# A decoder layer on one core: compressed probabilities copied earlier, the second scan a slot later, keys turned once, and another order of the first loads and weight splits

## The chip, the core and the metric

The kernel runs on one core of a Trainium2 chip. The core has a matrix engine (TensorE, "PE" in the profile; its weight loads are "PEld"), a vector engine (VectorE, "DVE"), a scalar engine (ScalarE, "ACT"), a general engine (GpSimd, "POOL") and a queue engine (SyncE, "SP"). The metric is device time in microseconds; the kernel before takes 485.9 us, the median of three runs.

## The reference

One layer of a hybrid decoder on x of 256 rows by 1024 columns, all in float32. An RMS norm, one wide projection, then two token mixers side by side: a gated linear recurrence behind a short convolution, and attention of 16 heads (64 columns each, 4 key groups) with three branches: compressed, selected and window. With 256 rows the selection takes all blocks, so the last two are two plain causal attentions with keys of their own. The mixers are merged by gates, projected, added to x, and a gated feed-forward follows.

```
h = rmsnorm(x, norm1[l]);  z = h @ w_in[l]
xr = causal_conv(z_rx, conv_w, conv_b)
xr = rg_lru(xr, ...)                 # h[t] = a[t] * h[t-1] + u[t], a scan over the rows
y_a = (xr * gelu(z_ry)) @ w_rg_out
k_s, k_w = rmsnorm(z_ks), rmsnorm(z_kw)
p_c = masked_softmax(q @ kc);  o_c = p_c @ vc        # compressed branch, 15 keys
p_s, p_w = the same over 256 keys each
o = g0 * o_c + g1 * (p_s @ v_s) + g2 * (p_w @ v_w)
x = x + (mg0 * y_a + mg1 * (o @ w_nsa_out)) @ w_o
x = x + (silu(h2 @ w_gate) * (h2 @ w_up)) @ w_down,  h2 = rmsnorm(x, norm2)
```

## The kernel before

All weights come as one stream of 73 slots of 128x2048 float32 (1 MB each), in the order of `ORDER`: rx 0 to 3, kk 4 and 5, rg 6 and 7, kc 8, vc 9, qa 10 and 11, qb 12 and 13, vv 14 and 15, ry 16 to 19, then mga, rgo, mgb, nso, wo, gu and dn. SP loads slot i into one of three `raw` buffers. ACT copies it rounded into `w_hi` (L369), DVE puts the remainder raw - w_hi into `w_lo` (L671), and PE makes three products per tile: high by high, high by low, low by high. Each engine's program is one loop over the slots, written out in order; nothing is scheduled by a tool. What the engines tell one another goes by semaphores: `landed`, `hi_ready`, `lo_ready`, `slot_done`, and for the eight PSUM banks `acc_free` (banks 0 to 3, projections) and `misc_free` (banks 4 to 7, transposes and attention).

**The start.** The rows of x come in two tiles of 128: tile 0 from SP's queue, tile 1 from ACT's. ACT squares and sums tile 0 (L375), DVE tile 1 (L679); DVE takes one mean for both (L676), POOL one power (L340), DVE scales both tiles into `xn` (L688). PE turns `xn` with 16 transposes (L1251). Ahead of them it transposes the identity 28 and 6 times (`keep_busy`, L1240), behind them 6 times. ACT writes the high part of the eight turned chunks (L389), DVE the low part (L720). The first slot of weights is loaded and split in two halves (L377 and L379 on ACT, L690 and L729 on DVE). PE's first product `first_x` (L1267 to L1269) takes chunk k as soon as its low part is there.

**The keys.** At slot 7 DVE normalises the keys and writes each 64-column key twice side by side (L892), so that the 16 transposes behind slot 7 (L1511) give keys on partitions 0 to 63 and again on 64 to 127. ACT and DVE then take high and low parts of all 128 partitions (L522, L943) into `k_hh` and `k_ll`. The scores need both copies, since a query holds its high part in the lower and its low part in the upper 64 partitions.

**The heads.** HEAD0 is slot 16; head h is handled at slot 16 + h and after. On PE, slot 16 + h begins with `scores(h)` (L1283). In the middle of its projection stand the transposes of the probabilities of head h - 1 (`turn_a` L1292, `turn_b` L1302); every second slot ends with `values(pair)` (L1319, L1323, L1326). DVE masks the scores and takes their maxima (L808, L811), ACT the exponentials (four, L473), DVE scales them (L844 to L850), and after PE has turned them ACT copies them back (L461, L463). The compressed branch of all heads is done once: scores in `first_y` at slot 16, softmax on DVE and ACT at slot 17, its transposes (L1200, `compressed_transposed`) in the middle of slot 18. ACT copies these into `pcT` (L481), and `values(0)` at the end of slot 18 waits for that copy. In ACT's order the copy stands behind the exponentials of head 2. The recurrence's scans of rows (L1012, four per half) stand on DVE at slot 13 and at slot 17 (`RG_SCAN`), at the end of the slot's work.

Of the kernel before, what the change touches and what calls it, by code (L numbers as in the profile page):

```python
# [59 lines left out]
MISC_ORDER = [("xT", 4), ("ng", 1), ("ngT", 1), ("kT", 4), ("hid", 1), ("kcn", 1), ("qTa", 2), ("vrep", 1), ("qTb", 2), ("att", 4 * HEADS), ("mT", 4), ("hT2", 4)]  # L60
# [12 lines left out]
RG_SCAN = (FIRST["qa"] + 3, FIRST["ry"] + 1)  # L73
# [17 lines left out]
def hybrid_layer(nc, x, stream, small_w, params, out):  # L91
    ctx = ExitStack()
    with ctx:
# [112 lines left out]
        x_in, x1_in, small_in, prm_in, x_again = sem("x_in"), sem("x1_in"), sem("small_in"), sem("prm_in"), sem("x_again")  # L206
# [16 lines left out]
        kn_ready, qn_ready = sem("kn_ready"), sem("qn_ready")  # L223
        sq_summed = sem("sq_summed")
# [11 lines left out]
        merged = sem("merged")  # L236
        x1_ready, silu_ready, a_prod, a_hi_ready, a_lo_ready = sem("x1_ready"), sem("silu_ready"), sem("a_prod"), sem("a_hi_ready"), sem("a_lo_ready")
# [24 lines left out]
        RS_BEFORE = [0, 1, 3, 5, 7, 8]  # L262
# [15 lines left out]
        def _(sp):  # L278
            sp.dma_start(xs[:, 0, :], x[0:P, :]).then_inc(x_in, 16)
# [32 lines left out]
        def _(pool):  # L312
# [45 lines left out]
        def _(sc):  # L358
            sc.dma_start(xs[:, 1, :], x[P:2 * P, :]).then_inc(x1_in, 16)
# [14 lines left out]
            sc.wait_ge(x_in, 16)  # L374
# [18 lines left out]
            chunks_hi(MISC["xT"], 0, G1)  # L393
# [29 lines left out]
            for i in range(NSLOT + 2):  # L423
# [93 lines left out]
                if i == FIRST["kk"] + 4:  # L517
                    for g in range(GROUPS):
                        m = MISC["kT"] + g
                        sc.wait_ge(misc_done, misc_count(m))  # L520
                        for b in range(2):
                            ins = sc.activation(k_hh[:, g, b * S:(b + 1) * S], misc(m)[:, b * S:(b + 1) * S], ACT.Copy,  # L522
                                                scale=prm[:, KN + 1 + b:KN + 2 + b])
                        ins.then_inc(evac_hi, 1)
# [133 lines left out]
        def _(ve):  # L658
# [23 lines left out]
            ve.wait_ge(dve_chain, chain[0])
            ve.wait_ge(squares, 1)
            mean(NORM_X, 1.0 / D)
            ve.wait_ge(rs_ready, rs_count(NORM_X))
            ve.wait_ge(x_in, 16)
# [40 lines left out]
            chunks_lo(MISC["xT"], 0, G1, 0, 4)  # L727
# [38 lines left out]
            for i in range(NSLOT + 2):  # L766
# [120 lines left out]
                if i == FIRST["kk"] + 3:  # L887
                    for t in range(T2):
# [49 lines left out]
                if i == FIRST["kk"] + 4:  # L938
                    for g in range(GROUPS):
                        m = MISC["kT"] + g  # L940
                        ve.wait_ge(evac_hi, g + 1)
                        for b in range(2):
                            ins = ve.scalar_tensor_tensor(out=k_ll[:, g, b * S:(b + 1) * S], in0=misc(m)[:, b * S:(b + 1) * S],  # L943
                                                          scalar=prm[:, KN + 1 + b:KN + 2 + b],
                                                          in1=f(k_hh[:, g, b * S:(b + 1) * S]), op0=ALU.mult, op1=ALU.subtract)
                        ins.then_inc(misc_free[m % 4], 1)
# [60 lines left out]
                for v in range(2):  # L1007
                    if i == RG_SCAN[v]:
# [4 lines left out]
                        link(ins)  # L1013
# [92 lines left out]
        def _(pe):  # L1106
# [531 lines left out]
```

## Time and profile before

| | us |
|---|---|
| median of 3 runs (485.82 to 485.99) | 485.9 |
| the profiled execution's own time | 487.44 |
| its span | 485.7 |
| PE busy in the span | 478.0 (98%) |
| DVE busy | 355.0 (73%) |
| ACT busy | 279.8 (58%) |
| POOL busy | 15.1 (3%) |

The profile is of one execution. Busy times are counted from the records, and PE's matmuls overlap one another, so that a busy PE does not say that nothing could be taken away. The granted clock of TensorE (PEclk) is given as a share of full speed.

### The profile page before, as it was taken

What the parts mean: (1) busy time and instruction counts of PE and PEld (TensorE: products, weight loads), DVE (VectorE), ACT (ScalarE), POOL (GpSimd) and SP (SyncE); (2) the same over time, 40 slices, a digit from 0 to 9 for tenths busy, and PEclk for the clock granted to TensorE, in tenths of its full rate; (3) what the DMA queues carried; (4) which work ended last, traced back from release to release, by engine and by line L of the source; (5) the groups of instructions that cost most, each with busy time, mean ns of one, the idle gap of its engine ahead of it and who ended that gap; (6) DMA issues with size and microseconds to landing.
All of it is one profiled execution on the core that took longest, in us unless ns stands there. A gap on an engine that the chain in (4) does not pass through costs nothing.

```text
span 485.7 us, 7347 instructions
## 1 busy us (share of the span) xinstructions
PE 478.0 (98%) x2803; PEld 412.7 (85%) x2803; DVE 355.0 (73%) x630; ACT 279.8 (58%) x451; POOL 15.1 (3%) x25
## 2 busy tenths in 40 slices
PE   7999999999989999999999999999999999999997
PEld 7998998788979778877787888888888888888886
DVE  3999899789895887757763767787777777754332
ACT  4755986675765896566763335755555445453320
POOL 2000200220000000000000000000000000000000
PEclk9999999999998999999999999999999999999999
DMA  8745966424224245333344362564555445554402
GB/s 311 272 162 208 373 271 255 174 88 173 88 97 164 88 173 194 152 128 135 106 154 165 104 251 88 188 246 177 187 206 209 175 173 181 200 224 175 173 1 86
DMA packets 12833, 84.73 MB, mean 174 GB/s; under 512 B 1536, under 2 KB 1792, under 8 KB 3072
## 3 DMA queue, kind: packets, MB, share of 16 engines
q1 hardware_dynamic: 12096, 82.32, 46.8%
q0 software_dynamic: 272, 1.05, 0.6%
q10 hardware_dynamic: 432, 0.91, 0.5%
q8 instruction: 22, 0.36, 0.3%
q14 instruction: 11, 0.09, 0.1%
HBM read 83.22 MB, written 1.05 MB: 173 GB/s over the span
## 4 chain that ended last, share of the span: by engine, by line
PE 93%; DVE 4%; ACT 2%; issue 0%; POOL 0%; POOLq 0%; DVEq 0%
PE bank L1109 18%; PE bank L1111 18%; PE bank L1110 18%; PE bank L1147 16%; PE bank L1150 8%; PE bank L1283 2%; PE bank L1319 2%; PE bank L1240 2%; PE bank L1521 1%; PE bank L1292 1%; DVE w_lo L671 1%; PE bank L1326 1%; PE bank L1323 1%; PE bank L1367 1%; ACT pbuf L473 1%; PE bank L1302 1%
## 5 line engine op out<-in xcount | busy, mean ns | idle before, releaser
L671 DVE TENSOR_TENSOR w_lo<-raw,w_hi 128x2048 fp32r<-128x2048 f32 x71 | 162.5, 2289 | 49.8 <-ACT w_hi L369 49.4
L369 ACT ACTIVATE w_hi<-raw 128x2048 fp32r<-128x2048 f32 x72 | 138.0, 1917 | 48.7 <-PE bank L1111 46.2
L1147 PE MATMUL bank<-h_hl,w_hi 128*128 128x512 f32 x336 | 80.3, 391 | 0.0
L1147 PEld LDWEIGHTS bank<-h_hl,w_hi 128*128 128x128 f32 x336 | 61.7, 188 | 11.9
L1109 PE MATMUL bank<-w_hi,h_hl 128*128 128x512 f32 x160 | 63.6, 398 | 0.0
L1111 PE MATMUL bank<-w_hi,h_hl 128*128 128x512 f32 x160 | 62.5, 390 | 0.0
L1110 PE MATMUL bank<-w_lo,h_hl 128*128 128x512 f32 x160 | 62.4, 390 | 0.0
L1109 PE MATMUL bank<-w_hi,act 128*128 128x512 f32 x150 | 59.1, 394 | 0.0
L1111 PE MATMUL bank<-w_hi,act 128*128 128x512 f32 x150 | 58.5, 390 | 0.0
L1110 PE MATMUL bank<-w_lo,act 128*128 128x512 f32 x150 | 58.4, 390 | 0.0
L1150 PEld LDWEIGHTS bank<-h_hl,w_lo 128*128 128x128 f32 x336 | 43.1, 191 | 1.6
L1150 PE MATMUL bank<-h_hl,w_lo 128*128 128x256 f32 x336 | 43.6, 283 | 0.0
L497 ACT ACTIVATE scr<-bank 128x512 f32<-128x512 f32 x22 | 13.1, 598 | 49.9 <-PE bank L1147 49.9
L1109 PE MATMUL bank<-h_hl,w_hi 128*128 128x256 f32 x128 | 36.6, 286 | 0.0
L1111 PE MATMUL bank<-h_hl,w_lo 128*128 128x256 f32 x128 | 36.2, 283 | 0.0
L1110 PE MATMUL bank<-h_hl,w_hi 128*128 128x256 f32 x128 | 36.2, 283 | 0.0
L1111 PEld LDWEIGHTS bank<-w_hi,h_hl 128*128 128x128 f32 x160 | 30.0, 188 | 6.5
L1109 PEld LDWEIGHTS bank<-w_hi,h_hl 128*128 128x128 f32 x160 | 30.1, 188 | 6.2 <-issue 0.4
L1110 PEld LDWEIGHTS bank<-w_lo,h_hl 128*128 128x128 f32 x160 | 30.1, 188 | 5.8
L1109 PEld LDWEIGHTS bank<-w_hi,act 128*128 128x128 f32 x150 | 28.2, 188 | 6.1 <-issue 0.4
L1111 PEld LDWEIGHTS bank<-w_hi,act 128*128 128x128 f32 x150 | 28.1, 188 | 6.0
L1110 PEld LDWEIGHTS bank<-w_lo,act 128*128 128x128 f32 x150 | 28.2, 188 | 5.6
(244 smaller groups left out, 744.6 us busy)
## 6 DMA issues: line engine op xcount, KB each, us to landing
raw<-stream_dram SPq DMA_DIRECT2D x72, 1024.0 KB, 4.8
w<-stream_dram SPq DMA_DIRECT2D x4, 1024.0 KB, 8.6
raw<-stream_dram SPq DMA_DIRECT2D x2, 512.0 KB, 7.3
xs<-x_dram POOLq DMA_DIRECT2D x1, 1024.0 KB, 5.4
out_dram<-xs SPq DMA_DIRECT2D x3, 256.0 KB, 2.0
xs<-x_dram ACTq DMA_DIRECT2D x1, 512.0 KB, 5.1
xs<-x_dram SPq DMA_DIRECT2D x1, 512.0 KB, 4.8
scr<-small_dram ACTq DMA_DIRECT2D x1, 320.0 KB, 8.8
```

The lines of the kernel that those rows point to most:

```text
L369: sc.activation(w_hi[:, i % HL, :], raw[:, i % RAW, :], ACT.Copy).then_inc(hi_ready, 1)
L473: ins = sc.activation(prob[:, a:b], bank[:, off:off + b - a], ACT.Exp, bias=ast[:, 1, j:j + 1], scale=SCALE, accum_out=ast[:, 2, j:j + 1])
L497: sc.activation(gus[:, j % 2, :, :], gate_up(j)[:, :, S:2 * S], ACT.Copy).then_inc(gu_low, 1)
L671: ve.tensor_tensor(w_lo[:, i % HL, :], raw[:, i % RAW, :], f(w_hi[:, i % HL, :]), ALU.subtract).then_inc(lo_ready, 1)
L1109: pe.matmul(out_, l_hi, r_hi, start=start, stop=False)
L1110: pe.matmul(out_, l_hi, r_lo, start=False, stop=False)
L1111: return pe.matmul(out_, l_lo, r_hi, start=False, stop=stop)
L1147: ins = pe.matmul(acc(u + mt)[:, :], w_hi[:, s, c:c + P], a_hl[:, k, :, :].rearrange("p x s -> p (x s)"), start=n == 0, stop=n == 2 * KC - ...
L1150: ins = pe.matmul(acc(u + mt)[:, 0:S], w_lo[:, s, c:c + P], a_hl[:, k, 0, :], start=n == 0, stop=n == 2 * KC - 1, skip_group_check=True)
L1240: pe.transpose(psum[3][:, 0:P], ident[:, :], ident[:, :])
L1283: ins = pe.matmul(o3, q, kt[:, g, :].rearrange("p (b c) -> p b c", b=2)[:, :, 0:w], start=n == 0, stop=n == 1)
L1319: pe.matmul(o[e], v_sb[:, 0, b * S + g * DH:b * S + (g + 1) * DH], pTa[e][:, b * S:(b + 1) * S], start=b == 0, stop=False)
```

## The change

Five things change. In ACT's order at slot 18 the copy into `pcT` moves ahead of the copies of the turned probabilities and of the exponentials. The second half of the scans moves from slot 17 to slot 18, with a semaphore `scanned` for which ACT's first copy of attention output waits (it writes over what the scan reads). The keys are no longer written twice: 8 transposes in place of 16, high and low parts on 64 partitions, and two transfers from POOL's queue that copy partitions 0 to 63 of `k_hh` and `k_ll` to 64 to 127; `scores(0)` waits for both. Each tile of x is loaded in two halves of 64 partitions, one from each queue, tile 0 first, and has a mean and a power of its own; tile 1's squares are summed half on DVE and half on ACT. The first half of the first weights is split in two quarters, the second half is copied by ACT between chunks 3 and 4 of the turned x, and only 2 identity transposes stand behind the transposes of x.

```
-MISC_ORDER = [("xT", 4), ("ng", 1), ("ngT", 1), ("kT", 4), ...
+MISC_ORDER = [("xT", 4), ("ng", 1), ("ngT", 1), ("kT", 2), ...
-RG_SCAN = (FIRST["qa"] + 3, FIRST["ry"] + 1)
+RG_SCAN = (FIRST["qa"] + 3, FIRST["ry"] + 2)
 # SP
-            sp.dma_start(xs[:, 0, :], x[0:P, :]).then_inc(x_in, 16)
+            for t in range(T2):
+                sp.dma_start(xs[0:64, t, :], x[t * P:t * P + 64, :]).then_inc(x_in[t], 16)
 # POOL
-            rsqrt(NORM_X)
+            for t in range(T2):
+                rsqrt(NORM_X, t, 1)
             for t in range(T2):
                 rsqrt(NORM_K, t, 8)
+            for g in range(2):
+                wait_misc_read(pool, MISC["kT"] + g)
+            for n, kt in enumerate((k_hh, k_ll)):
+                pool.dma_start(kt[64:128, :, :], kt[0:64, :, :]).then_inc(k_doubled[n], 16)
 # ACT
-            sc.dma_start(xs[:, 1, :], x[P:2 * P, :]).then_inc(x1_in, 16)
+            for t in range(T2):
+                sc.dma_start(xs[64:128, t, :], x[t * P + 64:(t + 1) * P, :]).then_inc(x_in[t], 16)
...
+            sc.wait_ge(x_in[1], 32)
+            sc.activation(scr[:, 3584:4096], xs[:, 1, 512:1024], ACT.Square, accum_out=ss[:, NORM_X, 2:3]).then_inc(x1_square, 1)
             sc.wait_ge(first_half, 16)
-            sc.activation(w_hi[:, 0, 0:1024], raw[:, 0, 0:1024], ACT.Copy).then_inc(hi_half, 1)
-            sc.wait_ge(landed[0], 16)
-            sc.activation(w_hi[:, 0, 1024:2048], raw[:, 0, 1024:2048], ACT.Copy).then_inc(hi_ready, 1)
+            for e in range(2):
+                sc.activation(w_hi[:, 0, e * 512:(e + 1) * 512], raw[:, 0, e * 512:(e + 1) * 512], ACT.Copy).then_inc(hi_half, 1)
...
-            chunks_hi(MISC["xT"], 0, G1)
+            chunks_hi(MISC["xT"], 0, G1, 0, 4)
+            sc.wait_ge(landed[0], 16)
+            sc.activation(w_hi[:, 0, 1024:2048], raw[:, 0, 1024:2048], ACT.Copy).then_inc(hi_ready, 1)
+            chunks_hi(MISC["xT"], 0, G1, 4, KC)
...
+                if i == HEAD0 + 2:
+                    u = USE["pcT"]
+                    sc.wait_ge(pcT_done, 1)
+                    sc.activation(pcT[:, :, :].rearrange("p a s -> p (a s)"), acc(u)[:, :], ACT.Copy).then_inc(acc_free[u % 4], 1)
                 if h >= 3 and h % 2 == 1 and h <= HEADS + 1:
                     pair = (h - 3) // 2
+                    if pair == 0:
+                        sc.wait_ge(scanned, 2)
 # DVE
-            ve.wait_ge(x1_in, 16)
-            ve.scalar_tensor_tensor(out=scr[:, 3072:4096], in0=xs[:, 1, :], ...
+            ve.wait_ge(squares, 1)
+            ve.tensor_scalar(ms[:, NORM_X, 0:1], ss[:, NORM_X, 0:1], 1.0 / D, EPS, ALU.mult, ALU.add).then_inc(ms_ready, 1)
+            ve.wait_ge(x_in[1], 32)
+            ve.scalar_tensor_tensor(out=scr[:, 3072:3584], in0=xs[:, 1, 0:512], ...
+            ve.wait_ge(x1_square, 1)
...
-            chunks_lo(MISC["xT"], 0, G1, 0, 4)
+            chunks_lo(MISC["xT"], 0, G1, 0, 2)
+            first_quarter(1)
+            chunks_lo(MISC["xT"], 0, G1, 2, 4)
...
-                        ve.tensor_tensor(kn[:, t, :].rearrange("p (c e d) -> p c e d", c=8, e=2),
-                                         kz[:, t, :].rearrange("p (c d) -> p c d", c=8).unsqueeze(2).broadcast_to([P, 8, 2, DH]),
+                        ve.tensor_tensor(kn[:, t, 0:512].rearrange("p (c d) -> p c d", c=8),
+                                         kz[:, t, :].rearrange("p (c d) -> p c d", c=8),
...
-                        link(ins)
+                        ins.then_inc(scanned, 1)
+                        ve.wait_ge(scanned, v + 1)
 # PE
-            keep_busy(6)
+            keep_busy(2)
...
                 for k in range(KC):
+                    if k == KC // 4:
+                        pe.wait_ge(lo_half, 2)
...
                 if h == 0:
                     wait_misc_read(pe, MISC["qTa"] + 1)
+                    for x in range(2):
+                        pe.wait_ge(k_doubled[x], 16)
```

The rows below are the engines' instructions in program order: the line, the operation, the tile written and the tiles read. ACT around the copy into `pcT` (slots 17 to 19), before; L434 and L448 belong to other work of these slots, L461 and L463 copy turned probabilities, L473 are exponentials, L369 is a weight copy:

```order
L369 ACTIVATE w_hi<-raw 128x2048
L434 ACTIVATE scr<-bank 128x512
L461 ACTIVATE pbuf<-bank 128x512
L463 ACTIVATE pbuf<-bank 128x256
L473 ACTIVATE pbuf,ast<-bank,ast 128x128 x2
L473 ACTIVATE pbuf,ast<-bank,ast 128x256 x2
L481 ACTIVATE pcT<-bank 128x512
L369 ACTIVATE w_hi<-raw 128x2048
```

The same place on ACT after the change (L379 is now the weight copy, L467 the copy into `pcT`, L493 the exponentials):

```order
L379 ACTIVATE w_hi<-raw 128x2048
L448 ACTIVATE scr<-bank 128x512
L467 ACTIVATE pcT<-bank 128x512
L481 ACTIVATE pbuf<-bank 128x512
L483 ACTIVATE pbuf<-bank 128x256
L493 ACTIVATE pbuf,ast<-bank,ast 128x128 x2
L493 ACTIVATE pbuf,ast<-bank,ast 128x256 x2
L379 ACTIVATE w_hi<-raw 128x2048
```

The copy into `pcT` moved up past four exponentials and two copies. DVE at slots 17 and 18 before: the weights' low part (L671), the scans (L1012), then the maxima of head 2 (L808, one instruction and one reading of its result per tile) and the rest of that slot:

```order
L671 TENSOR_TENSOR w_lo<-raw,w_hi 128x2048
L1012 SCALAR_TENSOR_TENSOR xs<-scr 128x256 x4
L808 ISA bank,ast<-bank,maskf 128x128
...
L811 TENSOR_SCALAR ast<-ast 128x4
L671 TENSOR_TENSOR w_lo<-raw,w_hi 128x2048
L844 RECIPROCAL ast<-ast 128x4
L845 TENSOR_TENSOR ast<-ast,gates 128x4
L850 TENSOR_SCALAR pbuf<-pbuf,ast 128x128 x2
L850 TENSOR_SCALAR pbuf<-pbuf,ast 128x256 x2
L808 ISA bank,ast<-bank,maskf 128x128
```

DVE at the same place after (L688 is the low part, L1042 the scans, L836 and L839 the maxima, L872 to L878 the scaling of the probabilities):

```order
L688 TENSOR_TENSOR w_lo<-raw,w_hi 128x2048
L836 ISA bank,ast<-bank,maskf 128x128
...
L839 TENSOR_SCALAR ast<-ast 128x4
L688 TENSOR_TENSOR w_lo<-raw,w_hi 128x2048
L872 RECIPROCAL ast<-ast 128x4
L873 TENSOR_TENSOR ast<-ast,gates 128x4
L878 TENSOR_SCALAR pbuf<-pbuf,ast 128x128 x2
L878 TENSOR_SCALAR pbuf<-pbuf,ast 128x256 x2
L1042 SCALAR_TENSOR_TENSOR xs<-scr 128x256 x4
L836 ISA bank,ast<-bank,maskf 128x128
```

The four scans moved from ahead of the maxima of head 2 to ahead of those of head 3. DVE at the start of the program before (L688 scales x, L690 and L729 are the low halves of the first weights, L720 the low parts of the turned chunks):

```order
L688 TENSOR_SCALAR scr<-xs,rs 128x1024 x2
L690 TENSOR_TENSOR w_lo<-raw,w_hi 128x1024
L720 SCALAR_TENSOR_TENSOR h_hl<-bank,prm,h_hl 128x256 x4
L729 TENSOR_TENSOR w_lo<-raw,w_hi 128x1024
L720 SCALAR_TENSOR_TENSOR h_hl<-bank,prm,h_hl 128x256 x4
```

DVE at the start after (L708 scales x, L713 are the quarters, L757 the second half, L746 the chunks):

```order
L708 TENSOR_SCALAR scr<-xs,rs 128x1024 x2
L713 TENSOR_TENSOR w_lo<-raw,w_hi 128x512
L746 SCALAR_TENSOR_TENSOR h_hl<-bank,prm,h_hl 128x256 x2
L713 TENSOR_TENSOR w_lo<-raw,w_hi 128x512
L746 SCALAR_TENSOR_TENSOR h_hl<-bank,prm,h_hl 128x256 x2
L757 TENSOR_TENSOR w_lo<-raw,w_hi 128x1024
L746 SCALAR_TENSOR_TENSOR h_hl<-bank,prm,h_hl 128x256 x4
```

The second quarter now stands between chunks 1 and 2. On ACT, in the same way, the copy of the second half of the first weights, which stood ahead of the eight chunks, now stands between chunk 3 and chunk 4.

## Rows read from the trace of the kernel before

**Rows 1.** The page's chain that ended last, shares of the span by engine.

```profile
PE 93%; DVE 4%; ACT 2%; issue 0%; POOL 0%; POOLq 0%; DVEq 0%
```

**Rows 2.** Waits of PE, 0 to 160 us: who waits for whom, total us, times, longest.

```profile
PE bank L1319 <- ACT pcT L481: 2.1, 1, 2.1
```

**Rows 3.** Timeline of PE, 130 to 160 us: start, us, engine, line, operation.

```profile
138.17 0.60 PE L1200 MATMUL bank<-ident,scr 128*128 128x128 f32 x4
...
142.02 0.28 PE L1111 MATMUL bank<-h_hl,w_lo 128*128 128x256 f32 x1
144.36 1.18 PE L1319 MATMUL bank<-pbuf,v_sb 128*64 128x256 f32 x8 [2.07 <-ACT pcT L481]
...
155.03 0.87 PE L1283 MATMUL bank<-act 128*128 128x256 f32 x4
```

**Rows 4.** Timeline of ACT, 130 to 160 us.

```profile
139.74 0.38 ACT L463 ACTIVATE pbuf<-bank 128x256 f32<-128x256 f32 x1
142.01 0.37 ACT L473 ACTIVATE pbuf<-bank,ast 128x128 f32<-128x128 f32 x1 [1.90 <-DVE ast L811]
...
143.61 0.61 ACT L481 ACTIVATE pcT<-bank 128x512 f32<-128x512 f32 x1
...
154.04 0.50 ACT L473 ACTIVATE pbuf<-bank,ast 128x256 f32<-128x256 f32 x1
```

**Rows 5.** Timeline of DVE, 130 to 160 us.

```profile
137.94 2.43 DVE L1012 TENSOR_TENSOR_SCAN xs<-scr 128x256 f32<-128x256 f32 x4
...
141.89 2.28 DVE L671 TENSOR_TENSOR w_lo<-raw,w_hi 128x2048 fp32r<-128x2048 f32 x1
...
144.49 1.01 DVE L850 TENSOR_SCALAR pbuf<-pbuf,ast 128x128 f32<-128x128 f32 x4
```

**Rows 6.** Stretches: length; busy of PE, PEld, DVE, ACT, POOL; PEclk; DMA.

```profile
144.36:148.80 4.44, 4.44 (x26) 3.47 (x27) 1.72 (x9) 2.53 (x3) 0.00 (x0) 0.62 0.59 240
162.04:164.84 2.80, 2.80 (x26) 2.10 (x26) 1.89 (x8) 2.80 (x10) 0.00 (x0) 1.00 0.78 260
```

**Rows 7.** Timeline of PE, 60 to 63 us.

```profile
60.24 1.91 PE L1511 MATMUL bank<-ident,scr 128*128 128x128 f32 x16
61.91 0.36 PE L1109 MATMUL bank<-h_hl,w_hi 128*128 128x256 f32 x1
```

**Rows 8.** The page's DMA issues: KB each, us from issue to landing.

```profile
w<-stream_dram SPq DMA_DIRECT2D x4, 1024.0 KB, 8.6
...
xs<-x_dram POOLq DMA_DIRECT2D x1, 1024.0 KB, 5.4
```

**Rows 9.** Timeline of SP, whole span, and of PE, 84 to 85 us.

```profile
66.12 0.91 SPq L296 DMA_DIRECT2D w<-stream_dram  x2
...
84.50 0.43 PE L1521 MATMUL bank<-w,pbuf 128*64 128x256 f32 x1
```

**Rows 10.** Timeline of PE, 2 to 18 us.

```profile
2.80 6.78 PE L1240 MATMUL bank<-ident 128*128 128x128 f32 x34 [2.80 <-POOL bd L331]
9.42 1.91 PE L1251 MATMUL bank<-ident,scr 128*128 128x128 f32 x16
...
12.00 0.36 PE L1267 MATMUL bank<-h_hl,w_hi 128*128 128x256 f32 x1
...
17.82 0.28 PE L1109 MATMUL bank<-h_hl,w_hi 128*128 128x256 f32 x1
```

**Rows 11.** Timelines of ACT and then of DVE, 0 to 130 us.

```profile
9.75 1.06 ACT L379 ACTIVATE w_hi<-raw 128x1024 fp32r<-128x1024 f32 x1 [0.84 <-DMA raw<-stream_dram]
10.78 3.03 ACT L389 ACTIVATE h_hl<-bank,prm 128x256 fp32r<-128x256 f32 x8
...
8.15 1.42 DVE L688 TENSOR_SCALAR scr<-xs,rs 128x1024 f32<-128x1024 f32 x2 [0.83 <-POOL rs L340]
...
11.37 1.66 DVE L720 SCALAR_TENSOR_TENSOR h_hl<-bank,prm,h_hl 128x256 fp32r<-128x256 f32 x4 [0.67 <-ACT h_hl L389]
12.95 1.21 DVE L729 TENSOR_TENSOR w_lo<-raw,w_hi 128x1024 fp32r<-128x1024 f32 x1
```

More of the change, by code:

```diff
@@ L205, in hybrid_layer @@
         landed = [sem(f"landed{i}") for i in range(RAW)]
-        x_in, x1_in, small_in, prm_in, x_again = sem("x_in"), sem("x1_in"), sem("small_in"), sem("prm_in"), sem("x_again")
+        x_in = [sem(f"x_in{t}") for t in range(T2)]
+        small_in, prm_in, x_again, x1_square = sem("small_in"), sem("prm_in"), sem("x_again"), sem("x1_square")
         hi_ready, lo_ready = sem("hi_ready"), sem("lo_ready")
@@ L236, in hybrid_layer @@
         merged = sem("merged")
+        scanned = sem("scanned")
         x1_ready, silu_ready, a_prod, a_hi_ready, a_lo_ready = sem("x1_ready"), sem("silu_ready"), sem("a_prod"), sem("a_hi_ready"), sem("a_lo_ready")
@@ L518, in _ @@
                     for g in range(GROUPS):
-                        m = MISC["kT"] + g
+                        m = MISC["kT"] + g // 2
+                        src = slice(64 * (g % 2), 64 * (g % 2) + 64)
                         sc.wait_ge(misc_done, misc_count(m))
                         for b in range(2):
-                            ins = sc.activation(k_hh[:, g, b * S:(b + 1) * S], misc(m)[:, b * S:(b + 1) * S], ACT.Copy,
-                                                scale=prm[:, KN + 1 + b:KN + 2 + b])
+                            ins = sc.activation(k_hh[0:64, g, b * S:(b + 1) * S], misc(m)[src, b * S:(b + 1) * S], ACT.Copy,
+                                                scale=prm[src, KN + 1 + b:KN + 2 + b])
                         ins.then_inc(evac_hi, 1)
@@ L676, in mean, with first_quarter @@
                 ve.tensor_scalar(ms[0:p, n, 0:w], ss[0:p, n, 0:w], scale, EPS, ALU.mult, ALU.add).then_inc(ms_ready, 1)
-            ve.wait_ge(x1_in, 16)
-            ve.scalar_tensor_tensor(out=scr[:, 3072:4096], in0=xs[:, 1, :], scalar=1.0, in1=xs[:, 1, :], op0=ALU.mult,
+            ve.wait_ge(squares, 1)
+            ve.tensor_scalar(ms[:, NORM_X, 0:1], ss[:, NORM_X, 0:1], 1.0 / D, EPS, ALU.mult, ALU.add).then_inc(ms_ready, 1)
+            ve.wait_ge(x_in[1], 32)
+            ve.scalar_tensor_tensor(out=scr[:, 3072:3584], in0=xs[:, 1, 0:512], scalar=1.0, in1=xs[:, 1, 0:512], op0=ALU.mult,
                                     op1=ALU.mult, accum_out=ss[:, NORM_X, 1:2]).then_inc(dve_chain, 1)
             chain[0] += 1
[L682 to L686, printed above, removed]
+            ve.wait_ge(x1_square, 1)
+            link(ve.tensor_scalar(ss[:, NORM_X, 3:4], ss[:, NORM_X, 2:3], 1.0 / D, EPS, ALU.mult, ALU.add))
+            ve.scalar_tensor_tensor(out=ms[:, NORM_X, 1:2], in0=ss[:, NORM_X, 1:2], scalar=1.0 / D, in1=ss[:, NORM_X, 3:4],
+                                    op0=ALU.mult, op1=ALU.add).then_inc(ms_ready, 1)
             for t in range(T2):
+                ve.wait_ge(rs_ready, rs_count(NORM_X, t))
+                ve.wait_ge(x_in[t], 32)
                 ve.tensor_scalar(xn[:, t, :], xs[:, t, :], rs[:, NORM_X, t:t + 1], None, ALU.mult).then_inc(xn_ready, 1)
-            ve.wait_ge(hi_half, 1)
-            ve.tensor_tensor(w_lo[:, 0, 0:1024], raw[:, 0, 0:1024], f(w_hi[:, 0, 0:1024]), ALU.subtract).then_inc(lo_half, 1)
+            def first_quarter(e):
+                ve.wait_ge(hi_half, e + 1)
+                ve.tensor_tensor(w_lo[:, 0, e * 512:(e + 1) * 512], raw[:, 0, e * 512:(e + 1) * 512],
+                                 f(w_hi[:, 0, e * 512:(e + 1) * 512]), ALU.subtract).then_inc(lo_half, 1)
+            first_quarter(0)
             ve.wait_ge(prm_in, 16)
@@ L939, in _ @@
                     for g in range(GROUPS):
-                        m = MISC["kT"] + g
+                        m = MISC["kT"] + g // 2
+                        src = slice(64 * (g % 2), 64 * (g % 2) + 64)
                         ve.wait_ge(evac_hi, g + 1)
                         for b in range(2):
[L943 to L946, printed above, removed]
+                            ins = ve.scalar_tensor_tensor(out=k_ll[0:64, g, b * S:(b + 1) * S], in0=misc(m)[src, b * S:(b + 1) * S],
+                                                          scalar=prm[src, KN + 1 + b:KN + 2 + b],
+                                                          in1=f(k_hh[0:64, g, b * S:(b + 1) * S]), op0=ALU.mult, op1=ALU.subtract)
+                        if g % 2 == 1:
+                            ins.then_inc(misc_free[m % 4], 1)
                 if i == FIRST["qa"] + 2:
@@ L1504, in _ @@
                     pe.wait_ge(kn_ready, 2)
-                    for g in range(GROUPS):
-                        m = MISC["kT"] + g
+                    for v in range(2):
+                        m = MISC["kT"] + v
                         wait_misc_free(pe, m)
```

19 lines of the change are left out of this document (8 added, 11 removed).

## The prediction

> **What bounds the kernel now.** First the page: the chain that ended last is PE for 93% of the span [rows 1], so only what shortens PE's own work or a wait of PE counts. Then PE's waits up to 160 us: beside the one at the very start a single one stands there, 2.1 us of L1319 for ACT's copy into `pcT` [rows 2]. Then the timelines around it. PE's last product of slot 18 starts at 142.02, the next instruction, `values(0)`, at 144.36 [rows 3]. ACT had finished the copies of turned probabilities at 140.12, waited 1.90 us for DVE's maxima of head 2, made four exponentials and only then copied `pcT` at 143.61 [rows 4]. DVE was late with the maxima because the four scans (2.43 us) stood ahead of them [rows 5]. Last the stretches: behind the wait the granted clock was 0.62 on the mean over 4.44 us, that is, part of it at 1.2 GHz in place of 2.4, and the values and scores took 4.44 us; the same group 18 us later took 2.80 us at clock 1.00 [rows 6].
>
> **The copy into pcT, and the scans.** The compressed transposes start at 138.17 and take 0.60 [rows 3], so `pcT` can be copied at 138.8. The copy takes 0.5 to the next start (143.61 to about 144.1, duration 0.61 [rows 4]) and ends before 139.4; the two copies behind it, which ended at 140.12, are put off by at most 0.1. PE then has all that `values(0)` needs at 140.2, and starts it right behind slot 18, at 142.02 + 0.12 = 142.14 (the first slot's 48 such matmuls take 17.82 - 12.00 = 5.82, 0.12 each [rows 10]). Gain: 144.36 - 142.14 = 2.2 us.
>
> Who is late next? `scores(3)` follows the values at 142.14 + 1.9 = 144.0 and needs the banks that the exponentials of head 2 read. Without the scans ahead of them the maxima end where the scans did, at 137.94 + (141.89 - 140.37) = 139.5; the exponentials start behind the copies at 140.2 and take 143.61 - 142.01 = 1.6 [rows 4, 5]: done at 141.8, 2.2 us early. Even at their old time of 143.6 they would be in time. So the first edit alone takes the wait away; the scans' move only makes it safe.
>
> What the move queues: DVE works on the next low part (2.2, from 139.5 to 141.7), scales the probabilities (1.01 [rows 5] and two small steps, 1.4 together by my estimate), done at 143.2, and scans until 145.6. Behind the scans stand the maxima of head 3, until 147.1. The exponentials of head 3 come only after PE has turned head 2 and ACT has copied it, at about 149.0, so 1.9 us are left. ACT's new wait for `scanned` holds its copy of attention output until 145.6 and ends it at 146.0; behind it are the copies of the turned probabilities at 148.2, and on PE `turn_b(2)` at about 148.0, which needs that copy. Both have 2 us. The tightest place is the usual one, the last exponential against `scores(4)`: in the old trace 154.54 against 155.03 [rows 3, 4]. Both shift together. Cost: nothing.
>
> **The clock.** With no gap at 142 there is nothing like what went before the drop. The stretch shrinks from 4.44 to 2.80 [rows 6]: gain 1.6 us. Bounds: 0 if the clock fell for another reason, 1.6 if it stays up. I take 1.6, as this is the only stretch with a low clock and it stands right behind the only gap.
>
> **Keys.** Of the 16 transposes behind slot 7, 1.67 us from start to next start [rows 7], 8 go: gain 0.83 us on PE, where nothing hides them. DVE writes half as much ahead of it, which costs nothing. The high and low parts keep their counts and row lengths; 64 partitions in place of 128 take as long or less. POOL waits for them and starts two transfers of 512 KB; behind it in its queue there are only the powers for q, two slots on. The parts are 16 operations of 0.4 at most behind transposes that end at 61, with other work between them, so I put the transfers at 70. They take 5.4 us by the one POOL transfer of the same total size [rows 8], and `scores(0)` wants them at slot 16, far behind the 84.50 of rows 9. They meet the stream there: two 1 MB loads issued at 66.12, first used at 84.50 [rows 9]. With the 8.6 us of such a load [rows 8] the second (issued at 67.0) lands at 76; if the doubled keys take all 5.4 us from it, at 81, and PE comes at 84.0. Cost: nothing, up to a delay of 8 us.
>
> Here the Trainium skill speaks against the change (SBUF — State Buffer, Door 1: The DMA port swizzle): the memory's DMA ports are divided by partition, and 64 partitions reach only half of them. An estimate by its figure of 436 GB/s for all is 218 GB/s, 4.8 us for the two. No run here shows such a transfer; it is within the 5.4 us taken above, and the sum is the same by either.
>
> **The start.** Tile 0 of x arrives earlier, and its scaled rows too, but does PE wait for them? It runs 34 identity transposes from 2.80 without a gap until the transposes of x at 9.42 [rows 10], while DVE began to scale at 8.15 and had tile 0 at about 8.9 [rows 11]. So PE's own 34 hold the place, they are all kept, and the earlier x is worth nothing. Behind the 16 transposes 4 of 6 go (0.44), which is no gain either, since PE then waits for the first low part. That comes from ACT's chunk 0 (10.78) over DVE (11.37) to PE (12.00), 1.22 us [rows 10, 11]. Chunk 0 waited for the second-half copy, to 10.81 [rows 11], and for the tenth of the 16 transposes (9.42 to 11.33), which ends near 10.7. So it starts at 10.71: 0.07 earlier.
>
> Then the chunks. ACT's go at 0.38 apart (3.03 for eight), DVE's at 0.41 (1.66 for four) [rows 11]. ACT: chunks 0 to 3 until 12.2, second half (1.0) until 13.2, chunk 4 at 13.2. DVE: chunks 0 and 1 from 11.30, second quarter from 12.1 (half of 1.21, so 0.6), chunks 2 and 3 from 12.7, second half 13.5 to 14.7, chunk 4 at 14.7 where before it came behind L729, at 14.1 [rows 11]. PE takes 0.73 per chunk (six matmuls): from 11.93 it comes to chunk 4 at 14.85, but that is ready only at 14.7 + 0.6 (12.00 - 11.37) = 15.3. It ends the slot at 18.2 in place of 17.8. Cost: 0.35 us, taken between the ends below as each step of it has a row. Slot 1 needs its first low half; ACT's copy (1.9) ends at 16.6 and DVE's half at 17.8, in time. ACT and DVE are about 0.9 later for the next slots too; what hides this is that PE waited for no low part anywhere before 142 [rows 2]. Bounds: -1.0 (the whole second-half copy, 1.06, off the way to the first product) to +1.06 (put wholly into it).
>
> **Sum.** -2.2 - 1.6 - 0.83 + 0.35 = -4.3 us. The profiled execution took 487.44 with a span of 485.7, so it should be 483.1 with a span of 481.4. The median of the runs is 1.5 below that execution: 485.9 - 4.3 = 481.6.
>
> **Rivals.**
> (a) The forecast, 481.6; its own range is 480.9 to 482.5. Chance 0.69.
> (b) The start gains in place of losing: ACT's idle time ahead of 9.75 was the real limit, the first product comes 0.8 earlier and the stall at chunk 4 is covered. For it: ACT did wait for a load there (0.84 us) [rows 11]. Against: PE's 34 transposes. -4.65 - 0.8 gives 480.4. Chance 0.11.
> (c) The clock falls somewhere else. The start now has two gaps of PE, 0.5 us ahead of the first product and 0.4 at chunk 4. If they bring one stretch at 1.2 GHz like the one at 144, +1.6: 483.2. Against: the old gap was 2.07 us. Chance 0.11.
> (d) Slower. The doubling of the keys crowds the loads of rows 9: if it delays them by more than 8 us, PE waits at 84 for each us more, and with a wait like the old one the clock drops too (1.6). It decides over the sign when PE waits 4.3 - 1.6 = 2.7 us, with the loads 10.7 us late; a doubling three times as slow as the POOL transfer (16 us) makes it 8 us of waiting: 8 + 1.6 - 4.3 = +5.3, so 491.2. Against: the 1 MB transfers of rows 8 took 5.4 and 8.6 us beside the stream. Chance 0.04.
> (e) The change doesn't do what it says: `values(0)` waits as long as before for something that I take as long done, the rest holds: -0.83 + 0.35 = -0.5, 485.4. The trace shows ACT's `pcT` as the last to come but not how close the second is. Chance 0.05.
>
> **How the numbers follow.** About 0.2% (1 us) is what a measurement of this kernel tells from no change. Faster by more: (a), (b) and (c), 0.91. Within: (e), 0.05. Slower: (d), 0.04. The range 480.2 to 483.8 holds (a), (b) and (c) with their bounds and leaves out (d), (e) and the outer ends of the start, under 0.2 together.
>
> **What would show it.** In the profile after: no wait of PE ahead of L1319 at slot 18, `pcT` copied at about 139 and ahead of the exponentials; PEclk 1.00 around 142 to 148; 8 key transposes in about 0.84 us; the transposes of x still at 9.42 and the first product near 11.9; a gap of 0.4 us in the first slot at chunk 4, and slot 1 starting 0.2 to 0.5 later than at 17.82. I am wrong if the transposes of x start well before 9.4, if a low clock stands anywhere, if PE waits at slot 19 or 20 for DVE's maxima, or if PE waits for `w1` near 84.

## The result and the profile after

The changed kernel takes 484.4 us (483.42 to 485.17, 12 executions). One more execution of it took 602.27 us at a mean granted clock of 0.755 and is left out as slow. Beside it the kernel before took 485.82 to 487.6 over 13 executions. The ratio is 0.9949, 95% interval 0.9937 to 0.9961: faster, by 1.9 to 3.1 us. The forecast was 481.6 with a range of 480.2 to 483.8, so the time lies outside it, 2.8 us above.

The first thing that the runs show is in the kernel before. Its times are not one group. Of its 57 executions beside the experiments below, 29 took 485.85 to 486.31 with a mean granted clock of 1.00, and 28 took 487.46 to 488.06 with 0.996; none lies between. The medians of the two kinds are 486.1 and 487.6. By their times, the three runs given at the outset were all of the first kind (median 485.9), and the profiled execution (487.44) was of the second. The interval above takes both kinds together; against the first kind alone the change gains 1.6 us.

| us | before | after |
|---|---|---|
| profiled execution, own time | 487.44 | 484.29 |
| its span | 485.7 | 482.5 |
| slot 1 begins | 17.82 | 19.08 |
| `values(0)` begins | 144.36 | 142.73 |
| stretch of values and scores ends | 148.80 | 145.58 |

Profile against profile the span is 3.2 us shorter, where 4.3 was forecast. The page's chain after, to be read beside [rows 1]:

```profile
PE 96%; DVE 1%; DMA 1%; ACT 0%; POOL 0%; issue 0%; ACTq 0%; DVEq 0%
```

All waits of PE in the changed kernel, over the whole span. The one of [rows 2] is gone; in its place are three short ones at the start, behind the 2.8 us that both kernels have:

```profile
PE bank L1271 <- POOL bd L335: 2.8, 1, 2.8
PE bank L1300 <- DVE h_hl L746: 0.7, 2, 0.5
PE bank L1282 <- DVE scr L708: 0.4, 1, 0.4
```

Timelines of the changed kernel around slot 18, of ACT, then DVE, then PE, each in a fence of its own; they answer to [rows 3 to 5]. `pcT` is L467, the exponentials L493, the maxima end with L839, `values(0)` is L1352 to L1359, the scores L1316:

```profile
139.31 0.60 ACT L467 ACTIVATE pcT<-bank 128x512 f32<-128x512 f32 x1 [1.54 <-PE bank L1231]
...
140.55 0.38 ACT L493 ACTIVATE pbuf<-bank,ast 128x128 f32<-128x128 f32 x1
...
146.19 0.38 ACT L475 ACTIVATE scr<-bank 128x256 f32<-128x256 f32 x1 [0.89 <-DVE xs L1042]
```

```profile
139.85 0.17 DVE L839 TENSOR_SCALAR ast<-ast 128x4 f32<-128x4 f32 x1
```

```profile
142.53 0.28 PE L1142 MATMUL bank<-h_hl,w_lo 128*128 128x256 f32 x1
142.73 1.08 PE L1352 MATMUL bank<-pbuf,v_sb 128*64 128x256 f32 x8
...
144.62 0.96 PE L1316 MATMUL bank<-act 128*128 128x256 f32 x4
145.42 0.28 PE L1140 MATMUL bank<-h_hl,w_hi 128*128 128x256 f32 x1
```

The values follow slot 18 directly, and ACT's new wait for the scans (0.89 us) holds nothing of PE. The stretch of values and scores took 4.44 us at clock 0.62 [rows 6] and takes 2.85 at 1.00 (columns as in [rows 6]):

```profile
142.73:145.58 2.85, 2.85 (x27) 2.16 (x27) 2.81 (x9) 2.40 (x2) 0.00 (x0) 1.00 0.75 253
```

The start is where the trace departs from the forecast. ACT, then DVE, of the changed kernel (L385 and L387 square tiles 0 and 1, L698 is DVE's half of tile 1, L708 scales):

```profile
5.25 1.06 ACT L385 ACTIVATE scr<-xs 128x1024 f32<-128x1024 f32 x1 [0.52 <-DMA xs<-x_dram]
8.02 0.64 ACT L387 ACTIVATE scr<-xs 128x512 f32<-128x512 f32 x1 [1.62 <-DMA xs<-x_dram]
```

```profile
8.02 0.69 DVE L698 SCALAR_TENSOR_TENSOR scr<-xs 128x512 f32<-128x512 f32 x1 [1.44 <-DMA xs<-x_dram]
9.06 0.75 DVE L708 TENSOR_SCALAR scr<-xs,rs 128x1024 f32<-128x1024 f32 x1
10.25 0.75 DVE L708 TENSOR_SCALAR scr<-xs,rs 128x1024 f32<-128x1024 f32 x1 [0.45 <-POOL rs L344]
```

And PE (L1271 identity, L1282 transposes of x, L1300 first product, L1140 slot 1):

```profile
2.80 6.66 PE L1271 MATMUL bank<-ident 128*128 128x128 f32 x34 [2.80 <-POOL bd L335]
9.87 2.29 PE L1282 MATMUL bank<-ident,scr 128*128 128x128 f32 x16 [0.40 <-DVE scr L708]
...
12.82 0.36 PE L1300 MATMUL bank<-h_hl,w_hi 128*128 128x256 f32 x1 [0.45 <-DVE h_hl L746]
...
16.13 0.36 PE L1300 MATMUL bank<-h_hl,w_hi 128*128 128x256 f32 x1 [0.20 <-DVE h_hl L746]
...
19.08 0.28 PE L1140 MATMUL bank<-h_hl,w_hi 128*128 128x256 f32 x1
```

The kernel before, where ACT had to do with tile 0 and DVE with tile 1, and POOL's first power of the changed kernel:

```profile
5.68 1.06 ACT L375 ACTIVATE scr<-xs 128x1024 f32<-128x1024 f32 x1 [2.17 <-DMA xs<-x_dram]
```

```profile
5.89 1.22 DVE L679 SCALAR_TENSOR_TENSOR scr<-xs 128x1024 f32<-128x1024 f32 x1 [5.89 <-DMA xs<-x_dram]
```

```profile
6.67 0.55 POOL L344 TENSOR_TENSOR rs<-ms,half 128x1 f32<-128x1 f32 x1 [3.92 <-DVE ms L696]
```

Tile 0 is usable at 5.25, a little before the old 5.7, but tile 1 only at 8.02, where before it was at 5.9. Tile 0's power is there at 7.2, yet DVE scales the tile only at 9.06, because tile 1's sum stands ahead of it in DVE's order and waits for tile 1. So the early tile 0 brings nothing. DVE has scaled tile 0 at 9.8 and tile 1 at 11.0, and PE is made to wait. Slot 1 starts 1.26 us later than in [rows 10], not 0.35.

### The profile page after: what moved, and what is told of

Read it like the earlier page. It is cut to its first block, busy times and chain, and to the rows that moved or that the text cites. A ratio compares the mean times of both kernels' runs of the same rounds, so it can differ in the third digit from the quotient of the medians.

```text
span 482.5 us, 7338 instructions
## 1 busy us (share of the span) xinstructions
PE 475.7 (99%) x2791; PEld 410.9 (85%) x2791; DVE 354.5 (73%) x633; ACT 280.7 (58%) x454; POOL 17.1 (4%) x28
## 4 chain that ended last, share of the span: by engine, by line
PE 96%; DVE 1%; DMA 1%; ACT 0%; POOL 0%; issue 0%; ACTq 0%; DVEq 0%
PE bank L1140 19%; PE bank L1141 19%; PE bank L1142 19%; PE bank L1178 16%; PE bank L1181 8%; PE bank L1316 3%; PE bank L1261 2%; PE bank L1352 2%; PE bank L1556 1%; PE bank L1325 1%; DMA xs<-x_dram 1%; PE bank L1400 1%; PE bank L1359 1%; PE bank L1335 1%; PE bank L1356 1%; DVE h_hl L746 0%
## 5 line engine op out<-in xcount | busy, mean ns | idle before, releaser
L688 DVE TENSOR_TENSOR w_lo<-raw,w_hi 128x2048 fp32r<-128x2048 f32 x71 | 162.5, 2290 | 49.5 <-ACT w_hi L379 49.1
L379 ACT ACTIVATE w_hi<-raw 128x2048 fp32r<-128x2048 f32 x72 | 138.0, 1917 | 47.9 <-PE bank L1142 41.5
L1140 PE MATMUL bank<-w_hi,h_hl 128*128 128x512 f32 x160 | 63.6, 398 | 0.0
L1140 PE MATMUL bank<-w_hi,act 128*128 128x512 f32 x150 | 59.1, 394 | 0.0
L513 ACT ACTIVATE scr<-bank 128x512 f32<-128x512 f32 x22 | 13.2, 598 | 49.9 <-PE bank L1178 49.9
L1140 PE MATMUL bank<-h_hl,w_hi 128*128 128x256 f32 x128 | 36.6, 286 | 0.0
L1140 PEld LDWEIGHTS bank<-w_hi,h_hl 128*128 128x128 f32 x160 | 30.1, 188 | 6.2 <-issue 0.4
L1140 PEld LDWEIGHTS bank<-w_hi,act 128*128 128x128 f32 x150 | 28.2, 188 | 6.1 <-issue 0.4
## 6 DMA issues: line engine op xcount, KB each, us to landing
act<-act POOLq DMA_DIRECT2D x2, 512.0 KB, 13.1
```

What stands on the lines that cost most here:

```text
L379: sc.activation(w_hi[:, i % HL, :], raw[:, i % RAW, :], ACT.Copy).then_inc(hi_ready, 1)
L513: sc.activation(gus[:, j % 2, :, :], gate_up(j)[:, :, S:2 * S], ACT.Copy).then_inc(gu_low, 1)
L688: ve.tensor_tensor(w_lo[:, i % HL, :], raw[:, i % RAW, :], f(w_hi[:, i % HL, :]), ALU.subtract).then_inc(lo_ready, 1)
L1140: pe.matmul(out_, l_hi, r_hi, start=start, stop=False)
```

## The experiments

The theory after the result: (1) two kinds of execution of the kernel before, with and without a fall of the clock behind the wait at 142; (2) the start costs 1.3 us, because a tile of x now comes in two pieces of 64 partitions. The rival to (1) is a gain that was smaller than forecast at slot 18, the rival to (2) is the new order of quarters and chunks. Each time is a median. The kernel before ran beside them in three sets, whose first kind has the medians 485.99, 486.07 and 486.07; sets of different kernels are compared on that ground. In the expectations, e1 is the copy alone, e4 all but the start, e6 the changed kernel with whole tiles of x, and e7 the same with halves by column.

**The copy into pcT alone.**

```
+                if i == HEAD0 + 2:        # now ahead of the exponentials
+                    u = USE["pcT"] ...    # the block that stood behind them
```

> The kernel before with one edit: the copy into pcT stands ahead of the exponentials on ACT in slot 18. The scans stay at the end of slot 17, keys and start are as before. Theory T (two modes): the kernel before is at 485.9 in executions whose clock stays up behind the wait at 142, and at 487.5 in those where it drops; this edit takes the 2.2 us wait and with it the drop. Both modes then come to one: 485.9 - 2.2 = 483.7 and 487.5 - 3.8 = 483.7, spread under 0.6. Rival U (the scans' move is needed too): DVE's maxima of head 2 still end at 141.9, the exponentials at 143.6, and scores(3) or a later head waits for them about 1 us: 484.7, with two modes left.

Measured: 483.92 (483.76 to 483.95), one group. Timeline of DVE, ACT and PE in this kernel, in three fences (L811 ends the maxima, L477 begins the exponentials, L1319 is `values(0)`, L1283 the scores):

```profile
141.82 0.17 DVE L811 TENSOR_SCALAR ast<-ast 128x4 f32<-128x4 f32 x1
```

```profile
138.82 0.60 ACT L453 ACTIVATE pcT<-bank 128x512 f32<-128x512 f32 x1 [1.54 <-PE bank L1200]
...
142.03 0.37 ACT L477 ACTIVATE pbuf<-bank,ast 128x128 f32<-128x128 f32 x1 [1.85 <-DVE ast L811]
```

```profile
142.24 1.08 PE L1319 MATMUL bank<-pbuf,v_sb 128*64 128x256 f32 x8
...
144.12 0.97 PE L1283 MATMUL bank<-act 128*128 128x256 f32 x4
```

The scans still stand ahead of the maxima and the exponentials are as late as before, yet nothing on PE waits for them: theory T, not U.

**The second scan alone.**

```
-RG_SCAN = (FIRST["qa"] + 3, FIRST["ry"] + 1)
+RG_SCAN = (FIRST["qa"] + 3, FIRST["ry"] + 2)
```

> The kernel before with the second scan alone a slot later (and ACT's wait for it); the copy into pcT stays behind the exponentials of head 2. Theory T (the copy's place is the cause, but the scans set when the exponentials end): the maxima of head 2 end at 139.6, the exponentials at 141.9, the copy into pcT at 142.5: PE waits about 0.4 us in place of 2.1 and the clock never drops: 484.3, one mode. Rival (the scans' move does nothing by itself, since ACT's exponentials wait for something else): 2.1 us of wait and both modes stay, 485.9 and 487.6.

Measured: 483.94 (483.94 to 484.1), one group, as good as the copy alone. Its rows of ACT and of PE (L484 is the copy, L1323 `values(0)`):

```profile
140.06 0.37 ACT L476 ACTIVATE pbuf<-bank,ast 128x128 f32<-128x128 f32 x1
...
141.64 0.63 ACT L484 ACTIVATE pcT<-bank 128x512 f32<-128x512 f32 x1
```

```profile
142.07 0.28 PE L1115 MATMUL bank<-h_hl,w_lo 128*128 128x256 f32 x1
142.41 1.08 PE L1323 MATMUL bank<-pbuf,v_sb 128*64 128x256 f32 x8
```

I had the copy 0.2 us too late; it ends at 142.27 and PE loses about 0.2. So each of the two edits by itself removes the wait, the scans' move all but these 0.2 us. No kernel with both and nothing else was run; what the scans' move adds to the copy can be bounded by the runs below at under 0.1 us.

**The wait filled.**

```
                 if pair == 0:
+                    for _ in range(18):
+                        pe.transpose(o_bank[:, 0:P], ident[:, :], ident[:, :])
```

> The kernel before with 18 transposes of the identity on PE where it waits for pcT in slot 18; their output is overwritten by the values behind them and changes nothing. They take about 18 x 0.11 = 2.0 us. Theory G (the idle stretch of PE is what precedes the drop of the clock, the late values by themselves are not): the 2.1 us stay lost, but the granted clock is 1.00 in each execution: 485.9 to 486.2, one mode. Rival (the drop comes with what runs at 144, or by chance): two modes, 486.0 and 487.6, about half of the executions each.

Measured: 486.09 (485.86 to 486.19), 12 executions, all at clock 1.00 (0.999 once). The kernel before fell to 0.996 in 9 of 17 beside it. PE, then the stretch of values and scores:

```profile
142.30 2.13 PE L1315 MATMUL bank<-ident 128*128 128x128 f32 x18
144.54 1.08 PE L1321 MATMUL bank<-pbuf,v_sb 128*64 128x256 f32 x8
```

```profile
144.30:148.80 4.50, 4.38 (x40) 3.77 (x39) 3.11 (x17) 2.66 (x4) 0.00 (x0) 1.00 0.71 233
```

The values are as late as before, but PE did not idle and the clock stays at 2.4 GHz. Without the idle stretch the fall does not come; theory G.

**The start alone, the keys alone, and all but the start.** The first two are the kernel before with one group of edits; the third has the copy, the scans and the keys, with the old start.

> The kernel before with the edits of the start alone (x tile by tile in halves of 64 partitions, the quarters, the second-half copy behind chunk 3, two rsqrts, keep_busy 2). Theory S (the start costs what the trace after shows): slot 1 starts at 19.1 in place of 17.82, +1.25 us: 487.1 where the clock stays up at 144 and 488.7 where it drops. Rival S0 (the start costs the 0.35 forecast, and the late slot 1 of the trace after is peculiar to that execution or caught up later): 486.2 and 487.8.

> The kernel before with the edits of the keys alone (8 transposes in place of 16, doubled by two transfers of POOL). Theory K (the doubling slows other loads, but PE hardly waits): 8 transposes save 0.88 us, behind them 0.4 us is lost until w1 at 84.5: -0.45 net, 485.4 or, with the drop at 144, 487.0. Rival K0: the full 0.88 stays, 485.0 or 486.6. Rival K1 (the doubling costs PE a wait at w1): slower than before by 0.5 or more.

> The changed kernel with the start of the kernel before (x in two whole tiles, two halves of the first weights, one rsqrt): pcT, scans and keys changed. Theory S: 484.44 - 1.25 = 483.2, slot 1 at 17.82, no wait of PE and clock 1.00 at 142 to 149. Rival S0: the start costs 0.35 and this gives 484.1. If terms add, it is also e1 plus the keys alone: 483.7 - 0.45 = 483.2.

Measured, start alone: 487.01; nine executions at 486.69 to 487.77 with clock 1.00, three at 488.42 to 488.48 with 0.996. Within the first kind it is 0.9 us slower than before (486.88 against 485.99), and its slot 1 starts at 19.07. Keys alone: 485.33; eight at 485.07 to 485.37, four at 486.79 to 487.01. Its profile (485.07) is of the first kind and shows the wait without the fall: PE, then the stretch of values and scores, which took 4.44 us at clock 0.62 in [rows 6]:

```profile
143.57 1.08 PE L1327 MATMUL bank<-pbuf,v_sb 128*64 128x256 f32 x8 [2.09 <-ACT pcT L486]
```

```profile
143.57:146.43 2.86, 2.86 (x26) 2.34 (x27) 1.53 (x8) 2.42 (x3) 0.00 (x0) 1.00 0.66 203
```

All but the start: 483.02 (482.87 to 483.52). Against the copy alone that is -0.90 for the keys and the scans' move together, and the keys alone give -0.83 (485.16 against 485.99, first kind). So the keys keep nearly all of the 8 transposes' 0.88, theory K0, and the scans' move adds under 0.1. The 0.4 us that I believed lost behind the transposes is not there. In the kernel without the new start PE comes to `w1` at

```profile
83.63 0.43 PE L1535 MATMUL bank<-w,pbuf 128*64 128x256 f32 x1
```

which is 0.87 ahead of [rows 9]. Beside the other edits the start costs 484.4 - 483.0 = 1.4 us, alone 0.9. The profiles of the changed kernel and of all but the start are 1.25 us apart at slot 1 (19.08 against 17.83) and 1.4 at `w1` (85.03 against 83.63). The profile of the start alone is 1.24 behind [rows 9] at `w1` (85.74) as well, but its execution is only 1.1 slower than the median of the first kind, and the median of its nine only 0.9. Where that difference comes from stays open. Theory S holds, S0 falls.

**Only the halves of x.** The kernel before, each tile of x in two transfers:

```
-            sp.dma_start(xs[:, 0, :], x[0:P, :])
+            for t in range(T2):
+                sp.dma_start(xs[0:64, t, :], x[t * P:t * P + 64, :])
                                               # and rows 64 to 127 on ACT's queue
```

> The kernel before with one edit: each tile of x comes in two halves of 64 partitions, one from SP's queue and one from ACT's; all else as before. Theory H (the half-tile transfers are what costs at the start): tile 1 is there at about 8.0 in place of 5.9, and the one rsqrt needs both tiles, so the scaled rows come 2.1 us later; 0.5 of that is covered by PE's identity transposes: slot 1 at about 19.4, +1.6 us, 487.6 where the clock stays up at 144. Rival O (the order of the chunks and quarters costs, not the transfers): 486.0.

Measured: 488.31, from 486.98 to 492.35; six at clock 1.00 have 486.98 to 487.85. PE in the profiled execution (490.73), and its stretches:

```profile
10.38 0.91 PE L1242 MATMUL bank<-ident 128*128 128x128 f32 x6 [1.95 <-POOL rs L341]
11.17 3.57 PE L1253 MATMUL bank<-ident,scr 128*128 128x128 f32 x16
```

```profile
10.30:14.60 4.30, 4.22 (x23) 4.07 (x24) 2.89 (x4) 1.99 (x4) 0.03 (x1) 0.60 1.02 423
```

The other six have 488.78 to 492.35 with clock 0.990 to 0.997. The transfers by themselves do the harm: +1.3 us where the clock stays up (the median of the six at 1.00 is 487.35). Behind the idle 1.95 us there is a second place where it can fall: here the 16 transposes took 3.57 us in place of 1.91 [rows 10]. Theory H, and a cost beyond it.

**Whole tiles, and halves by column.** The changed kernel; first with `xs[:, t, :]` in one transfer per queue, then with

```
-                sp.dma_start(xs[0:64, t, :], x[t * P:t * P + 64, :])
+                sp.dma_start(xs[:, t, 0:512], x[t * P:(t + 1) * P, 0:512])
                                               # and columns 512 to 1023 on ACT's queue
```

> The changed kernel with each tile of x in one transfer of 128 partitions (tile 0 on SP's queue, tile 1 on ACT's); quarters, order of chunks and two rsqrts as in the changed kernel. Theory H: tile 1 is there at 5.9 again, the transposes of x start at 9.4, slot 1 at 18.2: 483.4, with the small scatter of e4. Rival O: the late tile was covered and the order of chunks costs: slot 1 at 19 still, 484.3.

> The changed kernel with each tile of x in two transfers of 128 partitions by 512 columns in place of 64 partitions by 1024: the same two transfers of 256 KB on each of the same two queues. Theory H1 (the 64 partitions cost): as e6, tile 1 at about 6, 483.4. Rival H2 (the number of transfers ahead of the first weights, or both tiles standing in both queues, costs): tile 1 at about 8 as in the changed kernel, 484.4.

Measured: 483.05 (482.79 to 483.36) and 483.17 (482.68 to 483.46). The same stretch, 3 to 7 us, of before, the changed kernel, whole tiles, and column halves, one fence each; the last two columns are DMA share and GB/s:

```profile
3.00:7.00 4.00, 4.00 (x20) 4.00 (x20) 1.11 (x1) 1.67 (x3) 0.00 (x0) 1.00 0.96 350
```

```profile
3.00:7.00 4.00, 4.00 (x20) 4.00 (x20) 0.15 (x1) 2.43 (x3) 0.33 (x1) 1.00 1.02 231
```

```profile
3.00:7.00 4.00, 4.00 (x20) 4.00 (x20) 0.12 (x2) 1.82 (x4) 0.00 (x0) 1.00 0.97 353
```

```profile
3.00:7.00 4.00, 4.00 (x20) 4.00 (x20) 1.15 (x6) 2.88 (x5) 0.55 (x1) 1.00 0.98 316
```

In all four the DMA engines are busy throughout, but in the second they move a third less, in the fourth a tenth less. Two transfers of 256 KB on each queue are in both the second and the fourth; only the shape differs, so it is the 64 partitions (H1), not the number of transfers (H2) nor the order of the chunks (O). Nor is it the length of a row, which is 4 KB in the whole tiles too. A small part comes ahead of the transfer: to issue one took 0.56 to 0.85 us with 64 partitions and 0.40 to 0.47 with 128. By columns DVE has tile 1 as early as before:

```profile
5.92 0.69 DVE L698 SCALAR_TENSOR_TENSOR scr<-xs 128x512 f32<-128x512 f32 x1 [0.17 <-DMA xs<-x_dram]
```

With whole tiles the new start is worth nothing: 483.05 against 483.02 with the old one.

**Fewer identity transposes.** Column halves, and in front of x:

```
-            keep_busy(28)    # and 6 behind the first rsqrt
+            keep_busy(22)    # and 2
```

> The changed kernel with x in column halves (as e7) and 24 of PE's identity transposes ahead of x in place of 34. In e7 tile 0 of x is scaled by 7.7 and tile 1 by 8.9, but PE is at its identity transposes until 9.23. Theory I (PE's own transposes hold the start once x lands early): the 16 transposes of x end at 9.9 in place of 11.0, the first product comes at 10.8, slot 1 at 17.1 to 17.5, as the first weights' second half allows: 482.4 to 482.7. Rival J (the first weights' copies hold it): slot 1 stays at 18.0, 483.1. Rival C (the gap ahead of x drops the clock at the start in some executions): two modes, 482.6 and 484.0 or more.

Measured: 482.09, five executions: 481.82, 482.03, 482.09, 482.8 and 483.97. The profile is of the slowest. There PE turned x from 7.98, but then waited, because ACT had no weights:

```profile
11.85 0.36 PE L1300 MATMUL bank<-h_hl,w_hi 128*128 128x256 f32 x1 [1.60 <-DVE h_hl L746]
```

```profile
9.59 1.15 ACT L390 ACTIVATE w_hi<-raw 128x512 fp32r<-128x512 f32 x2 [3.17 <-DMA raw<-stream_dram]
```

Slot 1 began at 18.10 there, no earlier than with column halves alone (18.06), and a further wait of 0.64 us stands near 103, for DVE's `cmpr`. So J holds in that execution. Theory I fits the median, but of an execution as fast no trace was taken, so that its place is not shown. No clock below 0.999 was seen; the profiled execution kept 1.00 behind its 1.60 us of idle PE. It is the fastest version measured, 0.9901 of before (0.9883 to 0.9919), though its executions spread by 2 us.

## Why the prediction was wrong

Two steps failed. Together they are 1.6 + (1.4 - 0.35) = 2.65 of the 2.8 us.

**"The median of the runs is 1.5 below that execution: 485.9 - 4.3."** The sum was made against a profiled execution of 487.44 and carried over to a median of another kind. The clock term (1.6) was real, and its size was right: the medians of the two kinds differ by 487.6 - 486.1 = 1.5, and the stretch by 4.44 - 2.86 = 1.6. But it can be gained only from executions that lose it, and the three with median 485.9 had not. The 1.5 us between them and the profile was the term itself, in plain sight. Against 486 the copy saves 2.1 (483.92), against 487.6 it saves 3.7; both kinds end at 483.9.

**"... the earlier x is worth nothing ... Cost: 0.35 us."** The start was taken as a question of order, with x in its halves arriving no later than the whole tiles. The working never priced the four transfers, although it had a rule for them in hand. What the runs showed is 231 GB/s in place of 350, tile 1 at 8.02 in place of 5.9, and 1.4 us lost. The part that was worked out is about right: with x in column halves the first product comes at 11.81 and slot 1 at 18.06 (forecast 11.93 and 18.2), with the waits of 0.46 and 0.20 us at chunks 0 and 4. The bounds, up to +1.06, were drawn from ACT's copies and so missed the cause. The Trainium skill has it (SBUF — State Buffer, "Can I just issue two DMAs to hit both halves?"): a transfer to partitions from 0 and one to partitions from 64 issued together gain almost nothing over one, only a single transfer over all 128 reaches every port. By that page's 218 GB/s for 64 partitions (Door 1) the 1 MB of x is an estimated 4.8 us of transfer. The trace agrees: over 3 to 7 us, 231 GB/s in the changed kernel and 230 in the one with only the halves. I had weighed that section for the keys, where there was room, and not for x, where there was none.

The other steps:

- The wait: right. Gone, with the copy done early; the first edit alone takes it away (483.92), with the exponentials still at their old time and in time for `scores(3)`, as worked out. Not foreseen: the scans' move alone does as much (483.94). It was forecast as cover and is not needed for the gain.
- The keys: right. In the changed kernel 61.50 to 62.29 is 0.79 for 8 transposes, and the medians say 0.83. Wrong, without a cost: the eight high and eight low parts on 64 partitions took 3.38 and 3.78 us from first to last, where on 128 they took 3.01 and 3.22. The doubling is far off its 5.4 us, and rival (d) came closer than thought:

```profile
act<-act POOLq DMA_DIRECT2D x2, 512.0 KB, 13.1
```

  The loads of `w1` took 13.6 us beside it, where they took 9.4 before, and ACT once waited 3.95 us for weights at 87, but PE did not wait there. How much of the 13.1 is the 64 partitions and how much the crowd around it was not separated.
- Rival (b) fell. With x in whole tiles the first product does come 0.5 us earlier (11.53), but slot 1 begins at 17.78, where it did before.
- Rival (c), a clock that falls at the start, did not come: behind waits of 0.4 and 0.5 us the changed kernel stayed at 1.00 in all 12 executions. In the kernel with only the halves, with 1.95 us idle, it did. Rival (e) fell with the wait.

By medians over the first kind of execution the way from 486.0 to 484.4 is -2.1 (wait), -0.9 (keys and scans) and +1.4 (start). Each of these was measured on top of the one before, so that they add up by construction. Measured each on the kernel before they are -2.07, -0.83 and +0.89, which gives 484.0. The 0.4 us between is what the start costs more beside the other edits than alone, and its place stays open.

## What to carry to other kernels

Before a sum made on a profile is set against a median, ask what the difference between the two consists of: a term that explains it must not be subtracted again. Where a transfer is cut in two, cut it so that each piece still spans all 128 partitions; by 64 partitions it lost a third of the rate here and 1.4 us, by columns a tenth of the rate and no time that could be told from none. An idle stretch of PE costs more than its length when the clock falls behind it, so a gap that can't be closed may be filled with idle transposes. When parts measured one on top of the other add up, that is no check; measure each alone too.

## What the runs showed of the hardware

- Behind the same 2.1 us of idle PE the granted clock fell in 28 of 57 executions of the kernel before and in 7 of 24 with the start or the keys alone, and not in the others, at a price of 1.5 us by the medians. Filling the gap with transposes ended it (12 of 12). What decides in a given execution stays open.
- The pace of the 34 identity transposes at the start varies from one execution to the next. In the kernel with the wait filled, whose start is the old one, they span 6.02 us and the transposes of x begin at 8.72; in [rows 10] it is 6.78 and 9.42. With the old start this hardly reaches slot 1, which begins at 17.98 and 17.82. With the new start slot 1 follows it: 8.88 and 17.78 with whole tiles, 9.23 and 18.06 with column halves.

  ```profile
  2.81 6.02 PE L1240 MATMUL bank<-ident 128*128 128x128 f32 x34 [2.81 <-POOL bd L331]
  ```

- A transfer within the on-chip memory from 64 partitions to the other 64, two of 512 KB from POOL, took 12.2 to 13.2 us in the six kernels that have it, beside loads that kept the DMA engines full (in the changed kernel a DMA share of 0.97 to 1.12 from 70 to 85 us).
